# A decoder trunk on one core: two shuffle buffers on each side, and interleaved units in the down projections

## The reference

```python
def swiglu(h, w_gate, w_up, w_down):
    return (jax.nn.silu(h @ w_gate) * (h @ w_up)) @ w_down
...
    for l in range(DEPTH):
        x = x + 0.5 * swiglu(rmsnorm(x, norm_ffn1_g[l]), ffn1_w_gate[l], ffn1_w_up[l], ffn1_w_down[l])
        h = rmsnorm(x, norm_mix_g[l])
        proj = h @ w_in[l]
...
        x = x + merged @ w_out[l]
        x = x + 0.5 * swiglu(rmsnorm(x, norm_ffn2_g[l]), ffn2_w_gate[l], ffn2_w_up[l], ffn2_w_down[l])
    return rmsnorm(x, final_g)
```

## Time and profile before

| | us |
|---|---|
| median of 3 runs | 1120.84 (1120.32 to 1124.26) |
| the profiled execution | 1121.01 |
| its span, first to last instruction | 1119.0 |
| TensorE busy | 1081.6 (97%) |
| VectorE busy | 753.1 (67%) |
| ScalarE busy | 589.0 (53%) |
| GpSimd busy | 140.1 (13%) |

### The profile page before, as it was taken

One profiled execution on the slowest core, in us unless ns is written; L12 is line 12 of the kernel. 1 busy time (PEld: TensorE's weight loads), 2 busy tenths in 40 slices (PEclk: granted clock), 3 DMA queues, 4 the chain that ended last, 5 costly groups with the idle time before them and its releaser, 6 DMA issues.

```text
span 1119.0 us, 17635 instructions
## 1 busy us (share of the span) xinstructions
PE 1081.6 (97%) x5671; PEld 926.2 (83%) x5671; DVE 753.1 (67%) x952; ACT 589.0 (53%) x840; POOL 140.1 (13%) x258
## 2 busy tenths in 40 slices
PE   8999969999999999997999998999999999999897
PEld 7888758888899988886888887788888998888786
DVE  5665546768898866655676665568688987666554
ACT  6544434655585555444464453355567655554543
POOL 0233320000000012221002222000000000222200
PEclk9999989999999999998999999899999999999999
DMA  7878756555565678775677785656546656777662
GB/s 233 239 227 243 218 181 213 188 174 168 167 192 192 188 221 240 234 218 160 183 221 238 236 241 176 200 181 204 159 151 188 207 166 218 238 236 234 184 227 77
DMA packets 208899, 225.48 MB, mean 202 GB/s; under 512 B 16504, under 2 KB 194464, under 8 KB 208848
## 3 DMA queue, kind: packets, MB, share of 16 engines
q1 hardware_dynamic: 198160, 198.82, 57.6%
q0 software_dynamic: 10288, 25.48, 8.0%
q10 hardware_dynamic: 400, 0.51, 0.1%
HBM read 211.38 MB, written 13.37 MB: 201 GB/s over the span
## 4 chain that ended last, share of the span: by engine, by line
PE 58%; DMA 24%; POOL 7%; issue 5%; DVE 3%; ACT 3%; ACTq 0%; POOLq 0%; DVEq 0%
PE acc L1495 21%; DMA hid_scratch<-sum 13%; PE acc L1504 12%; DMA sum<-hid_scratch 11%; POOL hid_scratch L505 6%; PE acc L1499 4%; PE acc L1478 3%; PE acc L1476 3%; PE acc L1477 3%; DVE hm L1073 2%; ACT hm L698 2%; PE acc L1574 2%; PE acc L1577 2%; PE acc L1576 2%; POOL pars L518 1%
## 5 line engine op out<-in xcount | busy, mean ns | idle before, releaser
L958 DVE TENSOR_TENSOR w_lo<-raw,w_hi 128x1024 fp32r<-128x1024 f32 x382 | 450.7, 1202 | 156.0 <-ACT w_hi L596 155.2
L596 ACT CAST w_hi<-raw 128x1024 fp32r<-128x1024 f32 (+1 forms) x381 | 389.0, 1036 | 244.9 <-PE acc L1478 135.1
L1476 PE MATMUL acc<-w_hi,xm 128*128 128x512 f32 x688 | 268.8, 391 | 0.1
L1478 PE MATMUL acc<-w_lo,xm 128*128 128x512 f32 x688 | 267.8, 389 | 0.0
L1477 PE MATMUL acc<-w_hi,xm 128*128 128x512 f32 x688 | 267.8, 389 | 0.0
L1495 PE MATMUL acc<-hm,w_hi 128*128 128x512 f32 x528 | 173.0, 410 | 23.6 <-DVE w_lo L958 9.4
L1495 PE MATMUL acc<-xm,w_hi 128*128 128x512 f32 x576 | 183.1, 399 | 0.0
L505 POOL DMA_DIRECT2D hid_scratch<-sum x176 | 96.3, 554 | 486.8 <-DVE sum L1060 176.3
L1504 PEld LDWEIGHTS acc<-hm,w_lo 128*128 128x128 f32 x720 | 132.8, 194 | 24.9
L1476 PEld LDWEIGHTS acc<-w_hi,xm 128*128 128x128 f32 x688 | 129.2, 188 | 27.7 <-issue 1.4
L1478 PEld LDWEIGHTS acc<-w_lo,xm 128*128 128x128 f32 x688 | 129.1, 188 | 27.0
(11 more groups left out here) (186 smaller groups left out, 873.2 us busy)
## 6 DMA issues: line engine op xcount, KB each, us to landing
raw<-in_ffn_w_gate_dram SPq DMA_DIRECT2D x176, 256.0 KB, 3.3
raw<-in_ffn_w_up_dram SPq DMA_DIRECT2D x176, 256.0 KB, 3.9
raw<-in_ffn_w_down_dram SPq DMA_DIRECT2D x164, 256.0 KB, 3.6
raw<-in_w_in_dram SPq DMA_DIRECT2D x160, 256.0 KB, 3.3
hid_scratch<-sum POOLq DMA_DIRECT2D x176, 64.0 KB, 3.1
sum<-hid_scratch POOLq DMA_DIRECT2D x44, 256.0 KB, 3.0
raw<-in_w_out_dram SPq DMA_DIRECT2D x32, 256.0 KB, 3.0
raw<-in_w_branch_attn_dram SPq DMA_DIRECT2D x16, 256.0 KB, 3.1
```

The lines of the kernel that those rows point to most:

```text
L596: nc.scalar.copy(w_hi[:, s, 0:tiles, :], raw[:, s, 0:tiles, :]).then_inc(hi_split, 1)
L958: nc.vector.tensor_tensor(w_lo[:, s, 0:tiles, :], raw[:, s, 0:tiles, :], w_hi[:, s, 0:tiles, :], ALU.subtract).then_inc(lo_split, 1)
L1476: nc.tensor.matmul(s[:, t, :], xh, wh[:, k], start=not u and not k, stop=False, skip_group_check=True)
L1478: mm = nc.tensor.matmul(s[:, t, :], xh, wl[:, k], start=False, stop=(u, k) == (GU_UNITS - 1, GK - 1), skip_group_check=True)
```

## The change

turned and back become two buffers each: turned is sum0 or sum1, back the first or the second half of part, and there are two scratch tensors and two semaphores for the way back. GpSimd no longer waits for the DMA back at the end of a shuffle, and it waits for the remainder of the pair two sets back. The one-hot table that lay in part moves to v_tok. In three of the four down projections the first two column sets interleave: units 0 to 4 of set 0, 0 to 3 of set 1, 5 of set 0, 4 and 5 of set 1. The cast of the last pair of hidden tiles moves behind the weight cast of the unit with index 10. The loops over the down units are written out on SyncE and TensorE.

```diff
@@ the order of the down units
-DOWN_BODY = 2 * DOWN_UNITS
+DOWN_FIRST = ((0, range(0, DOWN_UNITS - 1)), (1, range(0, DOWN_UNITS - 2)), (0, range(DOWN_UNITS - 1, DOWN_UNITS)),
+              (1, range(DOWN_UNITS - 2, DOWN_UNITS)))
+DOWN_ORDER = [(j, k) for j, units in DOWN_FIRST for k in units] + \
+    [(j, k) for j in range(2, 2 * DOWN_ITERS) for k in range(DOWN_UNITS)]
+DOWN_HID = 10
...
@@ the buffers
-        turned = sums[0][:, :, :].rearrange("p k n -> p (k n)")
-        back = sums[1][:, :, :].rearrange("p k n -> p (k n)")
+        turned = [v[:, :, :].rearrange("p k n -> p (k n)") for v in sums]
+        back = [part[:, b * PAIR:(b + 1) * PAIR, :].rearrange("p k n -> p (k n)") for b in range(2)]
         hid_by_tile = hid.rearrange("p k (t n) -> p k t n", t=QT)
-        hid_dram = nc.dram_tensor("hid_scratch", (P, PAIR * SEQ), F32, kind="Internal").ap()
-
-        onehot = part[:, 0:PAIR, :].rearrange("p k n -> p (k n)")[:, 0:BIAS_LEN]
+        hid_dram = [nc.dram_tensor(f"hid_scratch{b}", (P, PAIR * SEQ), F32, kind="Internal").ap() for b in range(2)]
+
+        onehot = v_tok[:, 0, 0:BIAS_LEN]
...
+        hid_back = [sem(f"hid_back{b}") for b in range(2)]
...
+        def down_tiles(n):
+
+            return FT - UK * (DOWN_UNITS - 1) if n < len(DOWN_ORDER) and DOWN_ORDER[n][1] == DOWN_UNITS - 1 else UK
...
@@ SyncE
+            def downs(w, l):
+                for j, units in DOWN_FIRST:
+                    down(w, l, j * COLS, units)
+                for j in range(2, 2 * DOWN_ITERS):
+                    down(w, l, j * COLS)
...
-                with loop(sp, DOWN_ITERS, {split: DOWN_BODY}) as i:
-                    for j in range(2):
-                        down(ffn1_w_down, l, i * (2 * COLS) + j * COLS)
+                downs(ffn1_w_down, l)
...
@@ GpSimd
-            def shuffle():
-
+            def shuffle(k):
+
+                b = k % 2
                 shuffled.add()
                 written.add(16 * QUARTERS)
-                wait(pool, (hid_turned, shuffled.now), (hid_lo, shuffled.now - 1))
+                wait(pool, (hid_turned, shuffled.now), (hid_lo, shuffled.now - (2 if k else 1)))
...
                 wait(pool, (hid_out, written.now))
-                read.add(16)
-                pool.dma_start(back, hid_dram).then_inc(hid_back, 16)
-                wait(pool, (hid_back, read.now))
...
+                pool.dma_start(back[b], hid_dram[b]).then_inc(hid_back[b], 16)
...
@@ ScalarE (VectorE's loop is changed in the same way)
-                for i in range(2 * DOWN_ITERS):
-                    for k in range(DOWN_UNITS):
-                        u = k + LEAD
-                        hi(FT - UK * (DOWN_UNITS - 1) if u == DOWN_UNITS - 1 else UK)
-                        if i == 0 and u == 2 * LEAD - 1:
-                            rounded((GU_ITERS - 1) * PAIR)
-                    copy_acc(DOWN_UNITS)
-                    moving_x(i * PAIR, False)
+                done = 0
+                for n, (i, k) in enumerate(DOWN_ORDER):
+                    hi(down_tiles(n + LEAD))
+                    if n + LEAD == DOWN_HID:
+                        rounded((GU_ITERS - 1) * PAIR, 0)
+                    if k == DOWN_UNITS - 1:
+                        copy_acc(n + 1 - done)
+                        moving_x(i * PAIR, False)
+                        done = n + 1
...
@@ TensorE
-                with loop(pe, DOWN_ITERS, {unit: 12, sets: 2}):
-                    for _ in range(2):
-                        s = new_set()
-                        for n in range(DOWN_UNITS):
-                            tiles = range(n * UK, min((n + 1) * UK, FT))
-                            multiply(s, [hm[:, k, :] for k in tiles], n == 0, n == DOWN_UNITS - 1,
-                                     (hid_lo, hidden.now - (FT - 1 - tiles[-1]) // PAIR))
+                banks = {}
+                for j, n in DOWN_ORDER:
+                    if n == 0:
+                        banks[j] = new_set()
+                    tiles = range(n * UK, min((n + 1) * UK, FT))
+                    multiply(banks[j], [hm[:, k, :] for k in tiles], n == 0, n == DOWN_UNITS - 1,
+                             (hid_lo, hidden.now - (FT - 1 - tiles[-1]) // PAIR))
```

More of the change, by code:

```diff
@@ L432, in last_down, with down @@
                         slot[0] += 1
-            def down(w, l, col):
-                for k in range(0, FT, UK):
-                    load(rows(w, l)[:, k:min(k + UK, FT), bass.ds(col, COLS)])
+            def down(w, l, col, units=range(DOWN_UNITS)):
+                for k in units:
+                    load(rows(w, l)[:, k * UK:min((k + 1) * UK, FT), bass.ds(col, COLS)])
+            def downs(w, l):
[3 more added lines that the diff above has]
+                    down(w, l, j * COLS)
             def load_x(part_at, sem_at):
@@ L472, in _ @@
                     continue
-                with loop(sp, DOWN_ITERS, {split: DOWN_BODY}) as i:
-                    for j in range(2):
-                        down(ffn2_w_down, l, i * (2 * COLS) + j * COLS)
+                downs(ffn2_w_down, l)
             for t in range(QT):
@@ L519, in par @@
                                allow_slow_non_contiguous=True).then_inc(pars_loaded, 16)
-            shuffle()
+            shuffle(0)
             for n, v in enumerate((lambda_q1, lambda_k1, lambda_q2, lambda_k2)):
@@ L524, in _ @@
                     [P, DEPTH * HEAD_DIM])).then_inc(lam_loaded, 16)
-            shuffle()
+            shuffle(1)
             pool.wait_ge(lam_loaded, 64)
@@ L544, in _ @@
                                         1.0 - lambda_init(l), None, ALU.mult).then_inc(pars_ready, 1)
-            shuffles(GU_ITERS - 2 - 3 * DEPTH)
+            shuffles(2 + 3 * DEPTH)
             pool.wait_ge(bias_copied, 1)
@@ L563, in _ @@
             pool.wait_ge(bias_loaded, 32)
-            shuffles(GU_ITERS)
-            shuffles(GU_ITERS)
+            shuffles()
+            shuffles()
             pool.wait_ge(conv_ready, DEPTH)
@@ L689, in last_down, with rounded @@
                 stored(1)
-            def rounded(kt, moving=False):
+            def rounded(kt, b, moving=False):
                 hidden.add()
-                backs.add(16)
-                wait(act, (hid_back, backs.now))
+                backs[b].add(16)
+                wait(act, (hid_back[b], backs[b].now))
                 if moving:
                     act.reg_mov(spare, 0)
-                nc.scalar.copy(in_quarters(hm[:, at(kt), 0:SEQ]), tokens_last(back)).then_inc(hid_hi, 1)
+                nc.scalar.copy(in_quarters(hm[:, at(kt), 0:SEQ]), tokens_last(back[b])).then_inc(hid_hi, 1)
             def silu_of_set(*needs):
@@ L756, in gate_up @@
                     hi()
-                    rounded(kt, moving)
-                gate_up(0, False)
-                per = {split: 2 * GU_UNITS, loads: 64, sets: 2, units_done: 2 * GU_UNITS, hidden: 2, backs: 32}
+                    rounded(kt, b, moving)
+                gate_up(0, 0, False)
+                per = {split: 2 * GU_UNITS, loads: 64, sets: 2, units_done: 2 * GU_UNITS, hidden: 2,
+                       backs[0]: 16, backs[1]: 16}
                 with loop(act, (GU_ITERS - 1) // 2, per, 1) as i:
                     for n in range(2):
-                        gate_up(i * (2 * PAIR) + (n - 1) * PAIR, True)
+                        gate_up(i * (2 * PAIR) + (n - 1) * PAIR, 1 - n, True)
                 silu_of_set()
@@ L1092, in last_down @@
                     if u == LEAD + LEAD:
-                        remainder((GU_ITERS - 1) * PAIR)
+                        remainder((GU_ITERS - 1) * PAIR, 0)
                     if u == LAST_UNITS + LEAD:
@@ L1173, in ffn @@
                 lo()
-                hid_of_set()
+                hid_of_set(0)
                 lo()
@@ L1205, in ffn @@
                     nc.vector.tensor_copy(cur[:, :], pars[:, new_layer, :])
-                for i in range(2 * DOWN_ITERS):
-                    for k in range(DOWN_UNITS):
-                        u = k + LEAD
-                        lo(FT - UK * (DOWN_UNITS - 1) if u == DOWN_UNITS - 1 else UK)
-                        if i == 0 and u == 2 * LEAD - 1:
-                            remainder((GU_ITERS - 1) * PAIR)
+                for n, (i, k) in enumerate(DOWN_ORDER):
+                    lo(down_tiles(n + LEAD))
+                    if n + LEAD == DOWN_HID:
+                        remainder((GU_ITERS - 1) * PAIR, 0)
+                    if k < DOWN_UNITS - 1:
+                        continue
                     t = i * PAIR
```

49 lines of the change are left out of this document (24 added, 25 removed).

## The result

| | before | changed |
|---|---|---|
| median us | 1121.89 (1120.84 in the runs shown above) | 1080.55 (1080.14 to 1082.22) |
| profiled execution, its span | 1121.01, 1119.0 | 1080.56, 1078.8 |
| mean granted clock | 0.986 | 1.00 |

A forecast was written before the change was run, and what follows sets the result against it. TensorE's waits in the down projections and the lower clock behind them were taken to cost 38.3 us. 1121.0 - 38.3 = 1082.7, plus 0.5 us for each of three ties 1084.2, forecast 1084, range 1081 to 1096.

The forecast's parts named there:

- The ring: Around the down projections: shuffle, cast, remainder, next shuffle, one trip per pair of hidden tiles, 10.90 us, always a phase late.
- The sum of what is lost: TensorE's waits in the down projections, 27.5 us, plus the lower clock after them, 10.8 us: 38.3 us.
- The allowance for the ties: Unit 3 of the last three down projections, hidden tiles and TensorE arriving nearly together: 0.5 us left for each.
- The credit for the second waits: Waits of 3.14, 1.39 and 2.48 us in the first three down projections, said to go by moving units.
- GpSimd's wait for the trip back: Wait for the DMA back after each shuffle, removed by the change; given no size of its own.
- A longer shuffle (1): Shuffle longer than 9.0 us beside a busier weight stream; with 2 us more, 11 us lost, 1094; chance 0.15.
- Two close ends (2): Two column sets end too close: 3 x 1.1 us of waits, 1087.5, or with clock loss 1095; chance 0.10.
- Written-out code (3): TensorE's program fetched slower than it runs, waits at 3 x 24 down units; at 0.8 us each, 1140; chance 0.02.
- VectorE waiting for all DMAs (4): VectorE still waits for all earlier DMAs out before its transpose; only the units' move works, 1111; chance 0.03.
- The gap in GpSimd's issues: 1.14 us between two issues of one first-stage shuffle; if it came in each of three ties, 1086.1.

## Why the prediction was right, and where it failed

**The ring: right.** Shuffle, cast, remainder, next shuffle was the cause; opened, it took every wait of the earlier trace rows with it. The distance in the wait does most of it, not the buffer in itself (1073.9 against 1048.0), though without the second buffer a wait two sets back would have data overwritten, so the one is the price of the other. One row was misread: the transpose at 503.06 is that of set 10. Set 9's, the one at stake, was this:

```profile
493.46 0.71 DVE L1060 STREAM_TRANSPOSE sum<-ffn_store 128x512 f32<-128x512 f32 x1 [2.08 <-DMA hid_scratch<-sum]
```

Its shuffle then stood until 498.61 for the remainder. No term changes by it, for the sum starts at the multiply's end; from there to the shuffle it allows 1.2 us, and it took 1.04 (475.93 to 476.97).

**The sum of what is lost: too small, and this made the number and the range wrong.** The step that failed is that waits and clock loss, 38.3 us, are all that can be won ("below, 1081, for nothing else can be won"); 40.2 were won. Stage by stage the runs show 0.8 us up to the bias matmuls, 14.7 in the first down projection and 18.9 in the next two, and 5.8 in the last. By the rows that the prediction used, waits and clock, those are 0, 14.2, 18.4 and 5.7. So 0.8 us came from the first gate/up phase, where the matmuls' row has no idle time at all, though the row of the weight loads has small gaps in before:

```profile
79.52 0.19 PEld L1476 LDWEIGHTS acc<-w_hi,xm 128*128 128x128 f32 x1 [0.46 <-issue]
...
90.53 0.19 PEld L1476 LDWEIGHTS acc<-w_hi,xm 128*128 128x128 f32 x1 [0.25 <-issue]
```

TensorE loses time against the changed kernel at three places there, around 79.5, 90.5 and 101.6 us. VectorE's row ahead of the first:

```profile
77.58 0.71 DVE L1060 STREAM_TRANSPOSE sum<-ffn_store 128x512 f32<-128x512 f32 x1 [3.08 <-DMA hid_scratch<-sum]
78.22 2.32 DVE L958 TENSOR_TENSOR w_lo<-raw,w_hi 128x1024 fp32r<-128x1024 f32 x2
```

VectorE stands 3.08 us before its transpose, the first of the two weight remainders behind it ends at about 79.4, and TensorE, which waits for that remainder, goes on at 79.52. The other two places have the same order, with stalls of 2.97 and 3.07 us. From the mean square to the bias matmuls the kernel before took 107.4 us and every other kernel here 106.6 or 106.7. Among them are the one with nothing but the loads moved, the interleaving alone, whose ring is closed but which lacks the wait for the trip back, and the changed kernel with that wait. So the loss took all three: the closed ring, that wait, and the loads between the shuffles.

The other 1.1 us are about 0.16 for each wait, which is what the drawn matmul ends hide (0.39 - 0.23). A bound that rests on the idle times of TensorE's row is no bound.

**The allowance for the ties: too large.** 3 x 0.5 us were left for unit 3 in three stages, and some 0.15 was lost there in all; with the 1.9 us above this is 3.3 of the 3.5. How close the tie is differs with the execution: 0.1 us was lost at the shuffle of 9.18 us, nothing at those of 8.66 and 8.37. The forecast's 9.0 lies inside the 8.2 to 9.4 that were measured, so that it met one execution to 0.2 us is in part luck.

**The credit for the second waits: wrong part.** The prediction gave the 3.14, 1.39 and 2.48 us to the moved units. Its own working has the pair back at 12.5 us with unit 5 at 13.9, and cast and remainder take 1.3 us between them, which would have said that the open ring all but does it in the old order; I worked out the last unit's side only and did not ask. Measured with the buffers alone, the pair's cast starts 9.5 us after unit 0 (491.74 - 482.23). The sum did not suffer, since it counts these waits as gone whichever part takes them away; that is luck.

**GpSimd's wait for the trip back: missed.** It was treated as one more link of the ring. It makes a second ring, GpSimd's own, which closes only where the parameter loads lie between the shuffles: 9.1 us. The sum took all waits as gone, so this did not enter the number either.

**The rivals.** A longer shuffle (1) did not come: 9.18 us. Its price, 3.7 us for a wait of 2, was met by one wait, 1.99 + 0.29 x 5.95 = 3.7, and not by another: after 2.08 us, in the kernel before with early loads, the clock stayed at 1.00. Two close ends (2) did not wait here; moved closer still they cost 4.4 us in three stages, 1.5 each, against 1.1 in the prediction's working for the order as it is. Written-out code (3) is refuted by the run with loops, and VectorE waiting for all DMAs (4) by its 0.8 us of idle time before all transposes. The gap in GpSimd's issues came in the same place as before, in a shuffle of set 10, which is no tie:

```profile
135.29 1.64 POOL L516 DMA_DIRECT2D hid_scratch<-sum  x3 [1.13 <-issue]
```

It is 1.13 us here and 1.14 in the earlier trace rows; at 476.97 and 483.44 the four issues stay together in 2.19 and 2.18 us. By the Trainium skill, SBUF — State Buffer, section "SBUF: two separate sides", descriptor writes wait while VectorE, in a two-port mode, holds the shared ports. The trace rules that out for this gap: VectorE is idle all through it, from 133.30 to 136.69 us (DVE is the third engine of the row, at 0.00):

```profile
134.16:135.29 1.13, 1.13 (x8) 0.95 (x8) 0.00 (x0) 0.00 (x0) 0.00 (x1) 1.00 0.64 227
```

A larger gap, 2.31 us, stands in the first shuffle of the last feed-forward block (at 914.49; 2.43 in the kernel before), where TensorE does not wait. Both stand between the same two issues in all twelve traces in which GpSimd's loads lie between its shuffles. In the two with the loads moved, the first is gone, and one comes in the shuffle of set 9 in the second stage, a tie (here with the wait kept):

```profile
484.60 1.09 POOL L517 DMA_DIRECT2D hid_scratch<-sum  x2 [5.04 <-issue]
486.90 1.09 POOL L517 DMA_DIRECT2D hid_scratch<-sum  x2 [1.20 <-issue]
```

Its trip took 8.31 us, within the 8.2 to 9.4 of the others, and TensorE did not wait. In the kernel before with early loads it fell in the same shuffle, whose trip took 7.98 us where that kernel's others took 6.7 to 7.2. So the gap goes with GpSimd's program and not with VectorE's work, and in the one execution in which it fell in a tie it cost nothing; what makes it stays open.

## What to carry to other kernels

When a round trip takes about as long as the bottleneck engine's period, a buffer that must be back before the next trip starts costs phase rather than rate: the loop keeps step and is late only where something waits for the last round. Ask of each wait in the ring how many rounds back it needs to reach, and of each engine what else stands in its queue between two rounds. Run each half of a two-part change alone: here the buffers with the old order and loops do all of it, in less code.

## What was not expected of the hardware

- The time to the first mean square was 24.1 to 24.4 or 25.6 to 25.9 us in executions of kernels with the same start, and both in two executions of the changed kernel itself (24.4 and 25.9). This is more than the difference between it and the buffers alone, so executions were compared from there on.
- The length of a wait alone does not say what the clock does behind it. Waits of 1.56 and 1.65 us, and one of 2.08 us in the kernel before with early loads, left it at 1.00; waits of 1.99 and 2.16 were followed by 0.71 and 0.72, of 2.67 by 0.50. But in the kernel that waits one set back, 2.64 us left it at 1.00:

```profile
502.88 0.70 PE L1506 MATMUL acc<-hm,w_hi 128*128 128x512 f32 x2 [2.64 <-DVE w_lo L969]
...
502.88:508.88 6.00, 6.00 (x34) 5.25 (x35) 4.22 (x4) 2.50 (x3) 1.67 (x4) 1.00 0.88 255
```

- The trip through the scratch varies by a microsecond between executions and stages with nothing changed for it: 8.2 to 9.4 us with the ring open. In the kernel before, with the weight stream standing still, the trips of set 9 took 6.7 to 7.7 us.
- Loads that GpSimd issues at the very start of the program delayed the start-up by 3.9 and 7.3 us; what they collide with there was not looked into.
